# A decoder step with a mixture of experts: each expert block adds its gated rows to h by an accumulating scatter, and the closing stage keeps only the last norm

## The chip, the cores and the metric

One core of a Trainium2 chip runs the whole program. The metric is the device time of one execution in microseconds; the median of the runs counts. In the profile PE is the matmul engine (PEld its weight load), DVE the vector engine, ACT the scalar engine, POOL the GpSimd engine and SP the queue that issues plain DMAs; SPq, POOLq and so on are the instruction queues of these engines. L1835 is line 1835 of the kernel before.

## What is computed

The step is one decoder layer for 1,024 prompt tokens and 32 sample tokens (T = 1,056 rows of D = 1,024 float32), and a last norm. The part that the change touches is the mixture of experts and what follows it:

```python
def hier_moe(h, ...):
    ...
    top_v, top_i = lax.top_k(jax.nn.softmax(le, axis=-1), TOP_K)      # TOP_K = 2
    gate = g_p[:, None] * top_v / jnp.sum(top_v, axis=-1, keepdims=True)
    ...
    def expert_block(args):
        e, tok = args
        xb = x_pad[tok]
        hmid = jax.nn.silu(xb @ w_gate[e]) * (xb @ w_up[e])
        return hmid @ w_down[e]
    out = lax.map(expert_block, (blk_expert, buf_tok.reshape(n_blocks, MOE_BLOCK)))
    out = out.reshape(n_rows, D_MODEL) * buf_w[:, None]
    y = jax.ops.segment_sum(out, buf_tok, num_segments=n_tok + 1)[:n_tok]
    ...
h = h + hier_moe(rms_norm(h, norm_ffn_w), ...)
y_prompt, y_sample = rms_norm(h, norm_final_w)
```

Each token goes to 2 of 32 experts, which gives 2,112 assignments. An expert's rows are padded to blocks of 128, and the program makes at least one block for every expert; with these inputs there are 32 blocks (the trace shows 32 gathers and 32 scatters), so of 4,096 block rows 2,112 hold an assignment.

## The kernel before, in words

**Stages.** `front` (L129) computes everything up to the router: it stores h and its normed copy hn to DRAM scratch, and leaves on chip the gates (`S["gate"]`, 128 x 9 x 2), the one-hot choice of experts, each token's rank within its expert, and `S["place"]`, 18 matrices of 128 x 128 (one for each tile of 128 tokens and each of its two choices) that put an assignment on its row of a block. It also loads the first expert's weights. Then come `experts` (L1710) and `combine` (L2096). Between two such stages all engines meet at the end of a block of the program.

**The tables** are made at the start of `experts`. DVE works out in which block an assignment lies (`in_block`, 128 x 18 x 50), PE sums `place` times `in_block` over the 18 matrices (L1901, in the float32r type, one recorded matmul each), and the sum holds token + 1 in the rows of a first choice, -(token + 1) in those of a second, and 0 in an unfilled row. Seven DVE operations, six of them waiting for the one before (L2023 to L2030), turn this into two integer tables: row 0 the token to gather, with a number past the end for an unfilled row, and row 1 the row of `picked` to scatter to. L2032 copies the expert of every block. Each `table_ready` or `rows_ready` count lets the other engines go on.

**The loop over blocks.** The weights of an expert are 4 pieces `wgu` of 1 MB (gate and up) and 4 pieces `wd` of 0.5 MB (down). Every product is made of three float32r products, of high and low parts: ACT casts a piece to its high part (L1928, L1934), DVE subtracts to get the low part (L2048, L2057). There is one buffer for `wgu` and one for `wd`, so SP issues the load of the next expert's piece (L1785, L1792) when DVE has made the low part of the piece there. For a block i PE runs 48 matmuls of 512 columns for gate and up, turns the next block's tokens (L1859), runs 24 matmuls for down of block i - 1, and turns the hidden rows of block i (L1879). DVE copies the finished rows of block i - 1 from PSUM to `yb` (L2042, `unload_y`); PE may start the next down product only after that. The last block uses banks 4 and 5 and the tile `xg` in place of `yb` (L2088).

**GpSimd's queue** holds, in the order of the program: the gather of tokens for block i + 2 into `xg` (L1823 copies the column of row numbers to `src`, L1826 is the indirect DMA; it waits until PE has turned the tokens before), then the scatter of block i - 1 (L1832 copies the column to `dst`, L1835 is the indirect DMA from `yb` to the scratch tensor `picked`, 2T rows, one for each choice of each token). Row numbers past the end are skipped. The copy at L1832 waits until the scatter before has landed, and so does DVE's next write of `yb` (L2040).

**The end.** SP loads the last norm's weight and, while the last blocks compute, h itself: four tiles to `h_final` (L1804) and five to `h_late` (L1807). It waits for the last scatter (L1808), and the stage ends. `combine` then loads the two rows of each token from `picked` (L2126, nine DMAs, 8.65 MB), adds gate times row to h, for tiles 8, 0, 2, 4, 6 on DVE (L2186) and for tiles 1, 3, 5, 7 on PE with diagonal matrices of gates (L2209, L2148 to L2150), squares and sums on ACT (L2171 or L2165), takes the root (L2172, L2168), multiplies by its reciprocal and the weight on DVE (L2196, L2203, L2200), and stores from GpSimd's queue (L2134).

Of the kernel before, what the change touches and what calls it, by code (L numbers as in the profile page):

```python
# [6 lines left out]
ALU = mybir.AluOpType  # L7
# [3 lines left out]
I32 = mybir.dt.int32  # L11
# [1698 lines left out]
def experts(nc, A, S, C, bank):  # L1710
# [3 lines left out]
    with ExitStack() as ctx:  # L1714
# [44 lines left out]
        x_high, h_high = sem("xb_high"), sem("h_high")  # L1759
        silu_done, hid_ready = sem("silu_done"), sem("hid_ready")  # L1760
        xT_psum, xT_done = sem("xTb_psum"), sem("xTb_done")
        hT_psum, hT_done = sem("hT_psum"), sem("hT_done")
        y_done, y_stored = sem("y_done"), sem("y_stored")
# [10 lines left out]
        def _(sp):  # L1774
# [27 lines left out]
            sp.wait_ge(rows_ready, 1)  # L1802
            for j in range(FIRST):
                sp.dma_start(S["h_final"][:, j, :], S["h"][j * P:(j + 1) * P, :]).then_inc(S["final_loaded"][j], 16)  # L1804
            sp.wait_ge(gu_split, m * 4 + 8)
            for t in range(FIRST, NT + 1):
                sp.dma_start(S["h_late"][0:rows_of(t), t - FIRST, :], S["h"][t * P:t * P + rows_of(t), :]).then_inc(S["final_loaded"][t], 16)  # L1807
            sp.wait_ge(y_stored, m * 16 + 32)  # L1808
            sp.sem_inc(holder, 1)

        @block.gpsimd
        def _(pool):
# [4 lines left out]
                                    in_offset=bass.IndirectOffsetOnAxis(ap=of_row[:, 0, 0:1], axis=0),  # L1817
# [3 lines left out]
            def gather(i):  # L1821
                wait(pool, xg_loaded, i * 16)
                then_own(pool, nc.gpsimd.tensor_copy(src[:], of_row[:, 0, bass.ds(i, 1)]), src_ready, i)  # L1823
# [6 lines left out]
            def scatter(i):  # L1830
                wait(pool, y_stored, i * 16)
                then_own(pool, nc.gpsimd.tensor_copy(dst[:], of_row[:, 1, bass.ds(i, 1)]), dst_ready, i + 1)  # L1832
                pool.wait_ge(y_done, i + 1)
                pool.sem_inc(holder, 1)
                pool.indirect_dma_start(out=S["picked"], out_offset=bass.IndirectOffsetOnAxis(ap=dst[:], axis=0),  # L1835
                                        in_=yb[:], in_offset=None, bounds_check=2 * T - 1, oob_is_err=False).then_inc(y_stored, 16)

            gather(1)
            gather(2)
            with pool.Fori(1, m + 1) as i:  # L1840
                gather(i + 2)
                scatter(i - 1)
            scatter(m)
            scatter(m + 1)
            last = m + 2
# [484 lines left out]
```

## Time and profile before

| | us |
|---|---|
| median of 3 runs | 1507.23 (1505.0 to 1507.36) |
| profiled execution | 1505.11 |
| its span in the profile | 1503.4 |
| PE busy in the span | 1416.1 (94%) |
| DVE busy | 1061.5 (71%) |
| ACT busy | 766.1 (51%) |
| POOL busy | 568.4 (38%) |

The program's order in the span: `front` to about 861 us, the tables to 875 us, the loop over blocks to about 1456 us, the last scatter, and `combine` to the end. An engine's busy time doesn't count queue instructions. "DMA share" is the mean busy share of the core's 16 DMA engines; where packets overlap it can pass 1. "PEclk" is the matmul engine's granted clock as a share of full speed.

### The profile page before, as it was taken

To read this page: it belongs to the slowest core of one execution; us is meant where nothing else is said; L and a number is where in the kernel's file an instruction comes from. 1 tells how busy PE (TensorE), PEld (TensorE's weight loads), DVE (VectorE), ACT (ScalarE), POOL (GpSimd) and SP (SyncE) were. 2 spreads that over 40 slices of the span, in tenths; PEclk is the share of its full clock that TensorE was granted. 3 is DMA by queue.
4 is the path that set the end of the run, shared out by engine and by line. 5 is a ranking of instruction groups with operands and counts; after the bars stand their busy time and mean duration, and the time that the engine had idled before them with its cause. 6 is when DMAs were issued, how large, how long until landed. Compare 5 with 4: busy or idle time off the path is not lost. (4 is left out here: it accounts for less than half of the span.)

```text
span 1503.4 us, 21686 instructions
## 1 busy us (share of the span) xinstructions
PE 1416.1 (94%) x7625; PEld 1233.0 (82%) x7625; DVE 1061.5 (71%) x1225; ACT 766.1 (51%) x891; POOL 568.4 (38%) x345
## 2 busy tenths in 40 slices
PE   6999999999999999899999659999999999999976
PEld 5999999999999998788877548888888888888852
DVE  6687722366666664545463579999999999999956
ACT  6332222333333335344433438777777777777734
POOL 2323324454444442485644014333433333333311
PEclk9999999999999999999999669999999999999997
DMA  5222333234444445876653659999999999999958
GB/s 197 65 78 86 126 95 111 80 130 143 144 141 147 138 144 167 294 219 239 209 168 130 231 201 383 402 396 390 377 381 362 389 379 383 385 388 387 369 211 343
DMA packets 115793, 361.07 MB, mean 240 GB/s; under 512 B 18772, under 2 KB 48468, under 8 KB 99348
## 3 DMA queue, kind: packets, MB, share of 16 engines
q1 hardware_dynamic: 100164, 322.37, 58.6%
q0 software_dynamic: 15568, 37.87, 7.3%
q8 instruction: 41, 0.67, 0.2%
q14 instruction: 20, 0.16, 0.0%
HBM read 316.52 MB, written 59.64 MB: 250 GB/s over the span
## 5 line engine op out<-in xcount | busy, mean ns | idle before, releaser
L2048 DVE TENSOR_TENSOR wgu_l<-wgu,wgu_h 128x2048 fp32r<-128x2048 f32 x128 | 290.0, 2288 | 27.4 <-ACT wgu_h L1928 26.5
L1928 ACT CAST wgu_h<-wgu 128x2048 fp32r<-128x2048 f32 x124 | 237.4, 1915 | 100.6 <-PE bank0and L64 100.5
L62 PE MATMUL bank0and<-wgu_h,xh_blk 128*128 128x512 f32 x512 | 203.7, 398 | 2.9 <-DVE xl_blk L2052 2.9
L64 PE MATMUL bank0and<-wgu_h,xl_blk 128*128 128x512 f32 x512 | 200.9, 392 | 0.0
L62 PE MATMUL bank0and<-xh,wh 128*128 128x352 f32 x576 | 197.6, 343 | 3.0 <-ACT raw L906 3.0
L63 PE MATMUL bank0and<-wgu_l,xh_blk 128*128 128x512 f32 x512 | 200.3, 391 | 0.0
L64 PE MATMUL bank0and<-xh,wl 128*128 128x352 f32 x576 | 186.7, 324 | 0.0
L63 PE MATMUL bank0and<-xl,wh 128*128 128x352 f32 x576 | 186.5, 324 | 0.0
L1671 POOL TENSOR_TENSOR wol<-wo,woh 128x1024 fp32r<-128x1024 f32 x48 | 121.4, 2536 | 123.5 <-ACT woh L996 123.5
L1835 POOL DMA_INDIRECT scratch_picked<-yb,dst x31 | 92.7, 2991 | 197.5 <-DVE yb L2042 197.5
L2057 DVE TENSOR_TENSOR wd_l<-wd,wd_h 128x1024 fp32r<-128x1024 f32 x128 | 148.2, 1219 | 1.2 <-ACT wd_h L1934 1.0
L1622 POOL TENSOR_TENSOR wl<-w,wh 128x1024 fp32r<-128x1024 f32 x36 | 87.7, 2437 | 155.7 <-ACT wh L893 155.7
L1934 ACT CAST wd_h<-wd 128x1024 fp32r<-128x1024 f32 x128 | 124.9, 1049 | 1.7 <-PE bank2and L64 1.7
L62 PEld LDWEIGHTS bank0and<-wgu_h,xh_blk 128*128 128x128 f32 x512 | 96.8, 189 | 22.7 <-issue 2.8
L62 PEld LDWEIGHTS bank0and<-xh,wh 128*128 128x128 f32 x576 | 109.7, 190 | 6.9 <-issue 5.6
L64 PEld LDWEIGHTS bank0and<-wgu_h,xl_blk 128*128 128x128 f32 x512 | 96.6, 189 | 20.8
L63 PEld LDWEIGHTS bank0and<-wgu_l,xh_blk 128*128 128x128 f32 x512 | 96.9, 189 | 19.4
L63 PEld LDWEIGHTS bank0and<-xl,wh 128*128 128x128 f32 x576 | 110.0, 191 | 2.6 <-issue 1.9
L64 PEld LDWEIGHTS bank0and<-xh,wl 128*128 128x128 f32 x576 | 109.3, 190 | 0.0
L1191 DVE COPY stage<-bank2and 128x512 f32<-128x512 f32 x26 | 18.0, 692 | 123.3 <-PE bank2and L568 123.3
L915 ACT ACTIVATE feat<-bank0and 128x352 f32<-128x352 f32 x48 | 22.1, 463 | 156.1 <-PE bank0and L64 156.0
L62 PE MATMUL bank2and<-wd_h,hT_h 128*128 128x512 f32 x248 | 99.3, 401 | 0.0
(496 smaller groups left out, 3234.5 us busy)
## 6 DMA issues: line engine op xcount, KB each, us to landing
wgu<-in_w_gate_up SPq DMA_DIRECT2D x128, 1024.0 KB, 7.6
wd<-in_w_down SPq DMA_DIRECT2D x128, 512.0 KB, 7.6
wo<-in_w_out SPq DMA_DIRECT2D x48, 512.0 KB, 4.9
w<-in_w_in_tiles SPq DMA_DIRECT2D x36, 512.0 KB, 3.6
yy<-scratch_picked SPq DMA_DIRECT2D x8, 1024.0 KB, 12.6
scratch_xb<-stage POOLq DMA_DIRECT2D x10, 512.0 KB, 4.0
xb<-scratch_xb SPq DMA_DIRECT2D x8, 640.0 KB, 4.4
scratch_uT<-feat SPq DMA_DIRECT2D x8, 528.0 KB, 5.0
```

What stands on the lines that cost most here:

```text
L62: nc.tensor.matmul(acc, lh, rh, start=start, stop=False)
L63: nc.tensor.matmul(acc, lh, rl, start=False, stop=False)
L64: return nc.tensor.matmul(acc, ll, rh, start=False, stop=stop)
L915: nc.scalar.activation(feat[q % 2][:, b * TB:(b + 1) * TB], bank[b][:, 0:TB], func).then_inc(acc_free, 1)
L1191: ins = nc.vector.tensor_copy(stage[j][:, 4 * g:4 * g + 4, :], bank[3 + g][:].rearrange("p (t c) -> p t c", t=4))
L1622: nc.gpsimd.tensor_tensor(wl[q % 2][:], w[q % 2][:], wh[q % 2][:].bitcast(F32), ALU.subtract).then_inc(w_split, 1)
L1671: nc.gpsimd.tensor_tensor(wol[n % 3][:], wo[n % 3][:], woh[n % 3][:].bitcast(F32), ALU.subtract).then_inc(w_split, 1)
L1835: pool.indirect_dma_start(out=S["picked"], out_offset=bass.IndirectOffsetOnAxis(ap=dst[:], axis=0), in_=yb[:], in_offset=None, bounds_chec ...
L1928: nc.scalar.copy(wgu_h[:, s], wgu[:, s]).then_inc(gu_high, 1)
L1934: nc.scalar.copy(wd_h[:, p, :], wd[:, p, :]).then_inc(down_high, 1)
L2048: nc.vector.tensor_tensor(wgu_l[:, s], wgu[:, s], wgu_h[:, s].bitcast(F32), ALU.subtract).then_inc(gu_split, 1)
L2057: nc.vector.tensor_tensor(wd_l[:, p, :], wd[:, p, :], wd_h[:, p, :].bitcast(F32), ALU.subtract).then_inc(down_split, 1)
```

## The change

The second table and the scratch tensor `picked` go. h in DRAM gets 128 spare rows. One table of row numbers serves gather and scatter: token for a filled row, T + partition for an unfilled one. A table of gates for each row of each block is built beside it: DVE multiplies `in_block` by the gates (128 x 900), PE sums `place` times that over 18 float32 matmuls of 49 columns, and DVE divides by the token's signed number. GpSimd copies the column of gates of each block to `gate_of` (`copy_gate`), DVE multiplies by it where it copied before (`add_h`), and the scatter adds into h. All 128 rows of each block are written. `add_h` of the last block, which had waited for PE alone, also waits for the scatter before, and the last scatter too. After the last scatter SP loads h, nine tiles, and `combine` is square, root, reciprocal, product and store, with the stores on SP.

```diff
@@ experts: tiles
-        of_row = own("of_row", [P, 2, MAXBLK], I32)
+        of_row = own("of_row", [P, MAXBLK], I32)
+        gate_of, past_end = own("gate_of", [P, 1]), own("past_end", [P, 1])
+        gate_row = at("gate_row", 190208, [P, MAXBLK])
+        in_gate = at("in_gate", 182016, [P, N_ASG, WIDE])
@@ SP
-            sp.wait_ge(rows_ready, 1)
-            for j in range(FIRST):
-                sp.dma_start(S["h_final"][:, j, :], S["h"][j * P:(j + 1) * P, :]).then_inc(S["final_loaded"][j], 16)
             sp.wait_ge(gu_split, m * 4 + 8)
-            for t in range(FIRST, NT + 1):
-                sp.dma_start(S["h_late"][0:rows_of(t), t - FIRST, :], S["h"][t * P:t * P + rows_of(t), :]).then_inc(S["final_loaded"][t], 16)
             sp.wait_ge(y_stored, m * 16 + 32)
             sp.sem_inc(holder, 1)
+            for t in range(NT + 1):
+                sp.dma_start(S["h_final"][0:rows_of(t), t, :], S["h"][t * P:t * P + rows_of(t), :]).then_inc(S["final_loaded"][t], 16)
@@ GpSimd
+            def copy_gate(i):
+                wait(pool, y_done, i)
+                pool.sem_inc(holder, 1)
+                nc.gpsimd.tensor_copy(gate_of[:], gate_row[:, bass.ds(i, 1)]).then_inc(gate_copied, 1)
+
-            def scatter(i):
+            def scatter(i, rows=yb):
                 wait(pool, y_stored, i * 16)
-                then_own(pool, nc.gpsimd.tensor_copy(dst[:], of_row[:, 1, bass.ds(i, 1)]), dst_ready, i + 1)
+                pool.sem_inc(holder, 1)
+                then_own(pool, nc.gpsimd.tensor_copy(dst[:], of_row[:, bass.ds(i, 1)]), dst_ready, i + 1)
                 pool.wait_ge(y_done, i + 1)
                 pool.sem_inc(holder, 1)
-                pool.indirect_dma_start(out=S["picked"], out_offset=bass.IndirectOffsetOnAxis(ap=dst[:], axis=0),
-                                        in_=yb[:], in_offset=None, bounds_check=2 * T - 1, oob_is_err=False).then_inc(y_stored, 16)
+                pool.indirect_dma_start(out=S["h"], out_offset=bass.IndirectOffsetOnAxis(ap=dst[:], axis=0),
+                                        in_=rows[:], in_offset=None, bounds_check=T + P - 1, oob_is_err=True,
+                                        compute_op=ALU.add).then_inc(y_stored, 16)
             gather(1)
+            pool.wait_ge(table_ready, 3)
+            nc.gpsimd.tensor_copy(gate_of[:], gate_row[:, 0:1]).then_inc(gate_copied, 1)
             gather(2)
             with pool.Fori(1, m + 1) as i:
                 gather(i + 2)
                 scatter(i - 1)
+                copy_gate(i)
             scatter(m)
+            copy_gate(m + 1)
             scatter(m + 1)
-            last = m + 2
...
+            copy_gate(m + 2)
+            scatter(m + 2, xg)
@@ PE
+            pe.wait_ge(blk_ready, 2)
+            for a in range(N_ASG):
+                r = P if a < 2 * NT else TS
+                last = nc.tensor.matmul(bank[2][:, 0:MAXBLK], S["place"][0:r, a, :].bitcast(F32), in_gate[0:r, a, 0:MAXBLK], start=(a == 0), stop=(a == N_ASG - 1))
+            last.then_inc(blk_psum, 1)
             pe.wait_ge(rows_ready, 1)
             m = blocks_but_three(pe) + 1
             turn_x(0)
@@ DVE: the tables
+            after(nc.vector.tensor_scalar(past_end[:], C["row_no"][:], float(T + 1), None, ALU.add))
             dve.wait_ge(rows_psum, 1)
-            signed = of_row_f[:, 1, :]
+            signed, other, number = (of_row_f[:, j, :] for j in range(3))
             after(nc.vector.tensor_copy(signed, bank[0][:, 0:MAXBLK]))
...
+            after(nc.vector.tensor_scalar(other, signed, 0.0, past_end[:], ALU.is_equal, ALU.mult))
+            after(nc.vector.scalar_tensor_tensor(out=number, in0=signed, scalar=-1.0, in1=signed, op0=ALU.mult, op1=ALU.max))
+            nc.vector.scalar_tensor_tensor(out=of_row[:], in0=number, scalar=-1.0, in1=other, op0=ALU.add, op1=ALU.add).then_inc(rows_ready, 1)
             dve.wait_ge(blk_psum, 1)
             nc.vector.tensor_copy(blk_i[:, 0:MAXBLK], bank[1][0:1, 0:MAXBLK]).then_inc(table_ready, 1)
+            flat_gate = S["gate"][:].rearrange("p t k -> p (t k)")
+            nc.vector.tensor_tensor(in_gate[:], in_block[:].bitcast(F32), flat_gate.unsqueeze(2).to_broadcast([P, N_ASG, WIDE]), ALU.mult).then_inc(blk_ready, 1)
+            dve.wait_ge(rows_ready, 1)
+            after(nc.vector.tensor_scalar(other, signed, 0.0, None, ALU.is_equal))
+            after(nc.vector.tensor_tensor(other, other, signed, ALU.add))
+            after(nc.vector.reciprocal(other, other))
+            dve.wait_ge(blk_psum, 2)
+            nc.vector.tensor_tensor(gate_row[:], bank[2][:, 0:MAXBLK], other, ALU.mult).then_inc(table_ready, 1)
@@ DVE: the loop, and the last block
-            def unload_y(i):
+            def add_h(i, rows=yb, banks=S["banks23"]):
+                dve.wait_ge(gate_copied, i + 1)
                 wait(dve, y_stored, i * 16)
                 dve.wait_ge(down_used, i * 4 + 4)
-                nc.vector.tensor_copy(yb[:], S["banks23"][:]).then_inc(y_done, 1)
+                nc.vector.tensor_scalar(rows[:], banks[:], gate_of[:], None, ALU.mult).then_inc(y_done, 1)
...
-            dve.wait_ge(down_used, (m + 1) * 4 + 4)
-            nc.vector.tensor_copy(xg[:], S["banks45"][:]).then_inc(y_done, 1)
+            add_h(m + 1, xg, S["banks45"])
@@ combine: SP, ACT and DVE; what PE and GpSimd did goes
+            for t in range(NT + 1):
+                sp.wait_ge(out_ready, t + 1)
+                dst = A["y_sample"] if t == NT else A["y_prompt"][t * P:t * P + P, :]
+                sp.dma_start(dst, h[0:rows_of(t), t, :]).then_inc(out_stored, 16)
+            sp.wait_ge(out_stored, 16 * (NT + 1))
...
+                act.wait_ge(S["final_loaded"][t], 16 if t else 32)
+                after(nc.scalar.activation(junk[0:r, t % 2, :], h[0:r, t, :], ACT.Square, accum_out=st[0:r, t, 0:1]))
+                nc.scalar.activation(st[0:r, t, 1:2], st[0:r, t, 0:1], ACT.Sqrt, bias=C["eps"][0:r, :], scale=1.0 / D).then_inc(rms, 1)
...
+                dve.wait_ge(S["final_loaded"][t], 16 if t else 32)
+                dve.wait_ge(rms, t + 1)
+                after(nc.vector.reciprocal(st[0:r, t, 2:3], st[0:r, t, 1:2]))
+                nc.vector.scalar_tensor_tensor(out=h[0:r, t, :], in0=h[0:r, t, :], scalar=st[0:r, t, 2:3], in1=w[0:r, :],
+                                               op0=ALU.mult, op1=ALU.mult).then_inc(out_ready, 1)
@@ scratch
-    "h": (T, D), "hn": (T, D), "picked": (2 * T, D),
+    "h": (T + P, D), "hn": (T, D),
```

## Rows read from the trace of the kernel before

**Rows 1.** Busy time by stretch: span, busy us (instructions) of PE, PEld, DVE, ACT, POOL; PEclk, DMA share, GB/s.

```profile
1206.30:1312.60 106.30, 106.30 (x505) 88.47 (x504) 101.98 (x73) 80.71 (x67) 37.33 (x24) 1.00 0.99 382
1226.00:1229.54 3.54, 3.54 (x18) 2.92 (x17) 3.54 (x3) 2.23 (x2) 2.73 (x1) 1.00 1.03 418
1444.00:1450.00 6.00, 6.00 (x31) 4.95 (x29) 3.59 (x4) 4.13 (x5) 0.34 (x1) 1.00 1.02 415
...
1459.00:1503.40 44.40, 23.44 (x48) 10.01 (x48) 27.16 (x40) 15.80 (x40) 4.91 (x10) 0.73 0.77 299
```

**Rows 2.** DMA view of 1206.3 to 1312.6 us, six blocks: packets, MB, share of 16 engines.

```profile
DMA packets 8614, 40.63 MB, mean 382 GB/s; under 512 B 1744, under 2 KB 1744, under 8 KB 5566
...
q0 software_dynamic: 1728, 3.08, 7.6%
```

**Rows 3.** Timeline of POOL, one turn of the loop: start us, us, instruction, idle before.

```profile
1244.53 2.83 POOL L1835 DMA_INDIRECT scratch_picked<-yb,dst  x1 [6.50 <-DVE yb L2042]
1247.35 1.34 POOL L1823 COPY src<-of_row 128x1 int32 x1
1251.37 1.04 POOL L1826 DMA_INDIRECT xg<-scratch_hn,src  x1 [2.67 <-PE bank4and L1859]
1255.53 0.20 POOL L1832 COPY dst<-of_row 128x1 int32 x1 [3.12 <-DMA scratch_picked<-yb,dst]
```

**Rows 4.** Timeline of DVE, its next write of `yb` after that scatter.

```profile
1260.15 1.22 DVE L2042 COPY yb<-bank2and 128x1024 f32<-128x1024 f32 x1
```

**Rows 5.** Short float32 matmuls: busy time by stretch, timeline of the router's, durations of L1904.

```profile
863.00:876.00 13.00, 4.60 (x20) 4.14 (x20) 10.01 (x37) 0.00 (x0) 1.37 (x2) 0.50 0.00 2
...
848.07 3.63 PE L764 MATMUL bank0and<-w_router,hnT 128*128 128x36 f32 x16
...
L1904 PE MATMUL bank0and<-ident,blk_col x2: 238/257/276, 872.9 to 872.9; 49*1 49x49 f32 x2
```

**Rows 6.** Timeline from the tables to the first product of the loop.

```profile
866.17 0.78 DVE L1992 TENSOR_TENSOR in_block<-column_no,of_block 128x600 fp32r<-128x600 f32 x1
...
874.43 0.21 DVE L2030 CAST of_row<-of_row_f 128x98 int32<-128x98 f32 x1
...
875.71 6.70 DVE L2048 TENSOR_TENSOR wgu_l<-wgu,wgu_h 128x2048 fp32r<-128x2048 f32 x3 [0.97 <-DVE blk_i L2032]
...
883.08 1.23 DVE L2052 TENSOR_TENSOR xl_blk<-bank4and,xh_blk 128x1024 fp32r<-128x1024 f32 x1 [0.67 <-ACT xh_blk L1939]
...
884.45 0.77 PE L62 MATMUL bank0and<-wgu_h,xh_blk 128*128 128x512 f32 x1 [2.45 <-DVE xl_blk L2052]
```

**Rows 7.** Timeline of DVE and POOL at the last block, and a stretch after it.

```profile
1455.98 1.22 DVE L2088 COPY xg<-bank4and 128x1024 f32<-128x1024 f32 x1 [2.07 <-PE bank4and L64]
...
1458.05 0.97 POOL L1849 DMA_INDIRECT scratch_picked<-xg,src  x1 [4.10 <-DVE xg L2088]
...
1460.50:1461.00 0.50, 0.00 (x0) 0.00 (x0) 0.00 (x0) 0.00 (x0) 0.00 (x0) 0.50 0.33 131
```

**Rows 8.** The chain that ended last: its first DMA issue, its long transfer, its last issue.

```profile
1464.55 0.32 SPq L2126
...
1469.61 20.77 DMA yy<-scratch_picked
...
1499.12 0.53 POOL out_y_prompt L2134
```

**Rows 9.** The loads of h (ns min/median/max), then the timeline of ACT and DVE in `combine`.

```profile
L1804 SPq DMA_DIRECT2D h_final<-scratch_h x4: 423/444/707, 1438.9 to 1440.6; - x4
...
1474.29 1.28 ACT L2172 ACT_TABLE_LOAD   x1
1475.58 0.29 ACT L2172 ACTIVATE st_f<-st_f,eps 32x1 f32<-32x1 f32 x1
...
1476.95 0.29 ACT L2172 ACTIVATE st_f<-st_f,eps 128x1 f32<-128x1 f32 x1
...
1493.11 1.29 DVE L2203 SCALAR_TENSOR_TENSOR h_late<-h_late,st_f,w_final 128x1024 f32<-128x1024 f32 x1
```

More of the change, by code:

```diff
@@ L1759, in experts @@
         x_high, h_high = sem("xb_high"), sem("h_high")
+        gate_copied = sem("gate_copied")
         silu_done, hid_ready = sem("silu_done"), sem("hid_ready")
@@ L2075, in block_of @@
                 if not first:
-                    unload_y(i - 1)
+                    add_h(i - 1)
                 low_hid(i)
@@ L2123, in _ @@
         def _(sp):
-            for t in (8, 1, 0, 3, 2, 5, 4, 7, 6):
-                r = rows_of(t)
-                sp.dma_start(yy[t][0:r], S["picked"].rearrange("(k t) d -> t k d", k=2)[t * P:t * P + r]).then_inc(loaded[t], 16)
-        @block.gpsimd
-        def _(pool):
-            for n, t in enumerate(ORDER):
-                r = rows_of(t)
-                pool.wait_ge(out_ready, n + 1)
-                dst = A["y_sample"] if r == TS else A["y_prompt"][t * P:t * P + r, :]
-                pool.dma_start(dst, h[t][0:r, :]).then_inc(out_stored, 16)
-            pool.wait_ge(out_stored, 16 * (NT + 1))
-        def psum_of(t, half):
-            return bank[2 * (ON_PE.index(t) % 4) + half]
-        @block.tensor
-        def _(pe):
-            pe.wait_ge(diag_ready, 2 * len(ON_PE))
-            for n, t in enumerate(ON_PE):
-                pe.wait_ge(loaded[t], loaded_at[t])
-                for half in range(2):
-                    s = slice(half * 512, (half + 1) * 512)
-                    acc = psum_of(t, half)[:, :]
-                    nc.tensor.matmul(acc, C["ident"][:], h[t][:, s], start=True, stop=False)
-                    nc.tensor.matmul(acc, diag[:, n, 0, :], yy[t][:, 0, s], start=False, stop=False)
-                    nc.tensor.matmul(acc, diag[:, n, 1, :], yy[t][:, 1, s], start=False, stop=True).then_inc(pe_summed, 1)
+            for t in range(NT + 1):
[3 more added lines that the diff above has]
+            sp.wait_ge(out_stored, 16 * (NT + 1))
         @block.scalar
@@ L2265, in program @@
             S[name] = [ctx.enter_context(nc.semaphore(f"{name}{p}")) for p in range(parts)]
-        S["gu_high"] = ctx.enter_context(nc.semaphore("gu_high"))
+        for name in ("gu_high", "y_stored"):
+            S[name] = ctx.enter_context(nc.semaphore(name))
         front(nc, A, S, C, bank)
         S["w_final"] = at("w_final", 190464, [P, D])
-        S["h_final"] = at("h_final", 174080, [P, FIRST, D])
-        S["h_late"] = at("h_late", 0, [P, NT + 1 - FIRST, D])
-        late = [ctx.enter_context(nc.semaphore(f"f_loaded{t}")) for t in (4, 5, 7, 6)]
-        first = [ctx.enter_context(nc.semaphore(f"final_loaded{j}")) for j in range(FIRST)]
-        S["final_loaded"] = first + [late[0], late[1], late[3], late[2], first[1]]
+        S["h_final"] = at("h_final", 0, [P, NT + 1, D])
+        S["final_loaded"] = [ctx.enter_context(nc.semaphore(f"final_loaded{t}")) for t in range(NT + 1)]
         experts(nc, A, S, C, bank)
```

88 lines of the change are left out of this document (10 added, 78 removed).

## The prediction

> **What bounds the kernel now.** I read the busy time by stretch first, since the change touches three stages with different limits: the tables, the loop, the end. In the loop PE is busy for 106.30 of 106.30 us at the full clock [rows 1], so a block costs what PE's matmuls cost: six blocks in 106.3 us, 17.72 us each. But the DMA share in that row is 0.99, at 382 GB/s. I asked next whether the DMA engines have room. When they are plainly full (share over 1) they move 418 GB/s in the loop and 415 GB/s later, where both queues are mixed [rows 1]. Six blocks moved 40.63 MB, 6.77 MB each, of which the software queue (GpSimd's gathers and scatters) had 3.08 / 6 = 0.51 MB [rows 2]. At 418 GB/s 6.77 MB take 16.2 us. So the room is about 1.5 us a block, no more. That is the figure on which this change hangs.
>
> The end is another matter. From 1459 us the matmul engine matters little, and the chain that ended last runs from SP's issues at 1464.55 through the loads of `picked` (20.77 us) to the last store [rows 8]: this stage waits for its 8.65 MB.
>
> **The change, part by part.** The sum is made against the profiled execution, 1505.11 us, which is 2.1 us below the median of 1507.23.
>
> *Tables: +8.4 us.* Four chained DVE operations stand before `rows_ready` in place of seven. They take about 0.24 us each, so the row numbers are ready 0.7 us earlier than the end of the cast at 874.64 [rows 6]: 873.9. Then the copy of the experts (0.2), and the product of `in_block` with the gates: 600 elements took 0.78 us [rows 6], 900 about 1.1, which gives 875.2. PE now has 18 float32 matmuls, and they stand in its queue ahead of the turn of the first tokens. A float32 matmul is two records (L1904: one call, x2) and short ones take 3.63 / 16 = 0.227 us a record at the half clock, which is what PE was granted there [rows 5]. So 36 x 0.227 = 8.2 us, to 883.4. DVE's queue waits for their sum before `gate_row` (0.2), and behind that wait stand the three low parts that began at 875.71 after 0.97 us [rows 6]. They begin at about 884.6 and the low part of x follows at once, at 891.4 in place of 883.08: the 0.67 us for which it had waited for ACT is gone, as x is turned by 886. PE's first product starts then at 892.8 in place of 884.45 [rows 6], and every later step hangs on it: the weight loads of the next block wait for DVE's low parts. If the clock were at its full level, the matmuls would take half as long and the cost would be 4.3 us.
>
> *Loop, engines: 0.* DVE multiplies by a column instead of copying from PSUM, both 1,024 elements; I take 1.22 us for it too [rows 4], and DVE has 106.30 - 101.98 = 4.3 us idle in six blocks [rows 1] for a little more. GpSimd gets one more copy of a column, after the scatter, where a copy took 1.34 us; it then idled 2.67 us before the gather [rows 3]. The copy fits in that idle time. Were that cover gone, the gather would be late by 1.3 us, and it has several. `add_h` waits for a gate copied some 13 us before.
>
> *Loop, scatter: +0.37 us a block, the term that decides.* Before, a scatter wrote its filled rows only, 2,112 / 32 = 66 rows, 0.27 MB. Now all 128 rows are read from `yb` and written: 0.52 MB, that is 0.26 MB more. And each of these rows of h must be fetched from DRAM to be added to: 0.52 MB more. No row of the trace shows an accumulating DMA, so I bound it. Lower end: the fetch is free; 7.03 MB at 418 GB/s are 16.8 us, under 17.72, cost 0. Upper end: each fetched byte occupies the 16 engines as a loaded byte does, at the rate of the mixed stretch (415) with no better overlap than today: today 17.72 us hold 6.77 MB at a share of 0.99, so 7.55 MB could need 7.55 / 0.382 = 19.8 us, +2.0 a block. I take the fetched bytes as full ones, since they pass the same engines, and the full rate of the loop's own row: 7.55 MB / 418 GB/s = 18.09 us, +0.37 a block. The loads that compete run from the first scatter at about 926 us to the last `wgu` load at 1415, 28 blocks: +10.4 us.
> The Trainium skill, "Collectives: The Full Stack", section "The bandwidth ceiling: the fold count and why AG ≠ RS ≠ AR", says that a reducing transfer halves the rate because the add needs two source reads on one ring. By that rule the fetched bytes count in full, which gives the same sum; if a fetch were free the total would be 10 us lower. No row here shows it.
>
> *Scatter, landing: 0, with little margin.* DVE may write `yb` again when the scatter has landed. One scatter was issued at 1244.53 and had landed by 1255.53, 11.0 us later; the next write of `yb` came at 1260.15 [rows 3, 4]. So it may take 15.6 us. With twice the rows and the fetch (0.78 MB more over 16 engines that alternate with the weight loads: 1.9 us alone, some 3 in company) it lands after 13 to 14 us.
>
> *End: -12.5 us.* The last `add_h` must wait for the scatter before it, issued some 3.5 us ahead of the last copy at 1455.98 [rows 7]; with 128 added rows I let it start 1.3 us later. The last scatter was issued at 1458.05 and its data went until 1461.0 [rows 7]; its double volume and fetch add 1.3 us, so it lands at about 1464.0 in place of 1461.4. SP's next issue was at 1464.55 [rows 8], so leaving a stage cost 3.1 us. Now SP issues nine loads of h first, 0.44 us each [rows 9], to 1468.1, then 3.1 us: `combine` begins at 1471.2. The loads (4.3 MB, 10.4 us at 415 GB/s) keep ahead of ACT. ACT needs 1.37 us a tile (1475.58 to 1476.95) plus the table load of 1.28 once [rows 9]: first root at 1473.9. DVE then norms nine tiles at 1.29 us plus a short reciprocal, 1.4 each: 1486.5. The old end came 4.3 us after its last issue at 1499.12 [rows 8]; the same gives 1490.9 in place of 1503.4. The loads of `picked`, DVE's adds and PE's 48 matmuls are gone. The loads of h now lie open, where they had been hidden under the last blocks; that is in the sum.
>
> Together +8.4 + 10.4 - 12.5 = +6.3 us: 1511.4 for the profiled execution, 1513.5 against the median.
>
> **The rivals.** *A, the additions hide (faster).* If fetches are cheap, or the engines fill their gaps better than 418 GB/s says, the loop stays at 17.72 us and 8.4 - 12.5 = -4.1 is left: 1503. For it: 1.5 us of room, and the room needed is 0.6 (rows alone) to 1.9 us (rows and fetch). Against it: with the fetch the loop would have to average 426 GB/s, more than either full stretch [rows 1]. It decides from a transfer time of 17.72 us a block on.
> *B, the scatter lands too late (slower).* If an added row costs an engine a whole trip to DRAM that nothing overlaps, the landing passes 15.6 us, DVE waits for `yb`, and PE waits for it. Each microsecond beyond costs 30 us in all: 17 us would give 1503 + 42 = 1545. For it: only about 2 us of margin. Against it: eight rows for each engine are few.
> *C, the tables cost less.* If PE's clock rises during the 8 us of short matmuls, the tables cost 4 to 6 us. The stretch of short router matmuls at 848 us stayed at half clock to its end [rows 5], so I give it little. With the forecast's loop it gives 1510; with A's 1500.
> *D, it doesn't do what it says:* were unfilled rows still dropped as tiny packets, the loop would stay as it is, with A's time.
>
> **How the numbers follow.** A measurement of this kernel can tell about 0.2%, 3 us, from no change: below 1504.2 is faster, above 1510.2 slower. The forecast's own case (the loop grows by 0.1 to 0.8 us a block, 1506 to 1526) has 0.42, of which a quarter falls within 0.2%. A has 0.33 with D; of it 0.24 is faster, the rest within, as its -4.1 us is close to the bound. B, with the upper end of the transfer cost, has 0.18. C has 0.07, split over all. Faster 0.27, same 0.21, slower 0.52. The range goes from 1500 (A with a cheap table) to 1540 (the transfer at +1.2 us a block, or a landing of 17 us). Its own range for the likeliest case is 1506 to 1526.
>
> **What would show it.** The step between two writes of `yb`: 17.7 us for A, 18.0 to 18.5 for the forecast, with DMA share at 1.0 or over, and ACT's waits for weights (today for PE alone). For B: DVE idle before `add_h`, ended by the scatter. In the DMA view of six blocks the software queue should show at least 0.78 MB a block in place of 0.51, and fewer packets under 512 B. The first product of the loop should start at about 893 us, after 36 short matmul records that take 8 us. The stretch from the last product to the end should be 12 us shorter. The forecast is wrong if the loop's step is unchanged, or if GpSimd's gather makes PE wait.

## The result, and the profile after

The changed kernel took 1521.37 us (median of 4 runs, 1519.61 to 1522.66) against 1506.22 for the kernel before (4 runs). The ratio is 1.0100, with a 95% interval of 1.0082 to 1.0117: slower by 15 us. The profiled execution of the changed kernel spans 1519.6 us, 16.2 more than the 1503.4 of before. The direction was forecast and the time lies in the range, but the forecast had +6.3 us, less than half of what came.

I cut both executions at two points that every kernel of this study has: the start of the loop's first product (PE, L62) and the end of the last product of its last block (PE, L64; 1455.56 + 0.39 us in the kernel before).

| us | first product | loop, to the last product's end | from there to the end | span |
|---|---|---|---|---|
| before | 884.45 | 571.50 | 47.45 | 1503.4 |
| after | 891.71 | 592.46 | 35.43 | 1519.6 |
| difference | +7.26 | +20.96 | -12.02 | +16.2 |
| forecast | +8.4 | +10.4 | -12.5 | +6.3 |

So the miss is in the loop. These are three stretches of the changed kernel's busy time by stretch (columns as in [rows 1]), six blocks of the loop and two parts of the end:

```profile
1212.60:1325.20 112.60, 108.62 (x503) 87.80 (x503) 103.86 (x73) 81.41 (x67) 41.27 (x31) 1.00 1.03 376
...
1484.00:1496.00 12.00, 0.16 (x1) 0.00 (x0) 1.28 (x1) 0.00 (x0) 1.74 (x2) 0.71 0.46 79
1496.00:1519.60 23.60, 0.00 (x0) 0.00 (x0) 12.28 (x18) 13.39 (x28) 0.00 (x0) 0.50 0.94 367
```

Six blocks take 112.6 us in place of 106.3, and PE, which had been busy in all of them [rows 1], is idle for 4.0 us. The DMA share rose from 0.99 to 1.03, yet the engines move 376 GB/s where they moved 382. They are full, with less to show for it. The DMA view of 1239 to 1345 us in the changed kernel says which queue fills them:

```profile
DMA packets 8102, 39.99 MB, mean 377 GB/s; under 512 B 1242, under 2 KB 1242, under 8 KB 5199
...
q1 hardware_dynamic: 6603, 35.94, 83.3%
q0 software_dynamic: 1499, 4.06, 19.0%
...
wgu<-in_w_gate_up SPq DMA_DIRECT2D x22, 1024.0 KB, 14.3
wd<-in_w_down SPq DMA_DIRECT2D x24, 512.0 KB, 16.2
scratch_h<-yb,dst POOLq DMA_INDIRECT x6, 9.2
```

The software queue has 19.0% of the engines' time for 4.06 MB; before it had 7.6% for 3.08 MB [rows 2]. The bytes of rows fetched to be added to are not in this count. And the weight pieces take 14.3 and 16.2 us from issue to landing, in the kernel before 8.4 and 7.9 over the same stretch. The waits of ACT in the same stretch, in us, times, longest, show that they now land too late:

```profile
ACT wd_h L1947 <- DMA wd<-in_w_down: 15.7, 17, 1.5
ACT wgu_h L1941 <- DMA wgu<-in_w_gate_up: 13.3, 18, 1.0
```

In the kernel before, ACT waited at `wgu_h` for PE alone (20.7 us in six blocks, a buffer still in use). The loop's bound has passed from PE to the DMA engines. The step between two writes of `yb` says the same. This is the timeline of the changed kernel's DVE, two of its writes:

```profile
1243.41 1.28 DVE L2061 TENSOR_SCALAR yb<-bank2and,gate_of 128x1024 f32<-128x1024 f32 x1
...
1262.18 1.28 DVE L2061 TENSOR_SCALAR yb<-bank2and,gate_of 128x1024 f32<-128x1024 f32 x1
```

That is 18.77 us. The first three steps are still 17.7 us, the next ten 18.0 to 18.8, and the fifteen from 1168 us on 18.7 to 19.0: the loads start with a lead and lose it. The kernel before has 17.71 us from its third step on.

### The profile page after: what moved, and what is told of

The parts are those of the page before. It is cut to its first block and busy times, and to the rows that moved or that the text cites. A ratio compares the mean times of both kernels' runs of the same rounds, so it can differ in the third digit from the quotient of the medians.

```text
span 1519.6 us, 21757 instructions
## 1 busy us (share of the span) xinstructions
PE 1410.4 (93%) x7613; PEld 1231.0 (81%) x7613; DVE 1057.6 (70%) x1206; ACT 769.2 (51%) x879; POOL 567.1 (37%) x368
## 3 DMA queue, kind: packets, MB, share of 16 engines
q0 software_dynamic: 14368, 41.66, 11.3%
## 5 line engine op out<-in xcount | busy, mean ns | idle before, releaser
L62 PE MATMUL bank0and<-wgu_h,xh_blk 128*128 128x512 f32 x512 | 204.6, 400 | 16.9 <-DVE xl_blk L2071 16.9
L64 PE MATMUL bank0and<-wgu_h,xl_blk 128*128 128x512 f32 x512 | 201.0, 393 | 0.0
L62 PE MATMUL bank0and<-xh,wh 128*128 128x352 f32 x576 | 197.5, 343 | 2.9 <-ACT raw L906 2.9
L64 PE MATMUL bank0and<-xh,wl 128*128 128x352 f32 x576 | 186.6, 324 | 0.0
L1947 ACT CAST wd_h<-wd 128x1024 fp32r<-128x1024 f32 x128 | 133.3, 1053 | 72.2 <-DMA wd<-in_w_down 67.5
L2076 DVE TENSOR_TENSOR wd_l<-wd,wd_h 128x1024 fp32r<-128x1024 f32 x128 | 153.4, 1223 | 12.2 <-ACT wd_h L1947 11.3
L1842 POOL DMA_INDIRECT scratch_h<-yb,dst x31 | 58.9, 1901 | 207.7 <-DVE yb L2061 207.7
L62 PEld LDWEIGHTS bank0and<-wgu_h,xh_blk 128*128 128x128 f32 x512 | 96.8, 189 | 42.1 <-DVE xl_blk L2071 15.3
L62 PEld LDWEIGHTS bank0and<-xh,wh 128*128 128x128 f32 x576 | 109.5, 190 | 6.9 <-issue 5.5
L64 PEld LDWEIGHTS bank0and<-wgu_h,xl_blk 128*128 128x128 f32 x512 | 97.0, 189 | 20.8
L64 PEld LDWEIGHTS bank0and<-xh,wl 128*128 128x128 f32 x576 | 109.2, 190 | 0.0
L62 PE MATMUL bank2and<-wd_h,hT_h 128*128 128x512 f32 x248 | 99.3, 401 | 0.0
```

Source lines behind the costliest of these rows:

```text
L62: nc.tensor.matmul(acc, lh, rh, start=start, stop=False)
L64: return nc.tensor.matmul(acc, ll, rh, start=False, stop=stop)
L1842: pool.indirect_dma_start(out=S["h"], out_offset=bass.IndirectOffsetOnAxis(ap=dst[:], axis=0), in_=rows[:], in_offset=None, bounds_check=T ...
L1947: nc.scalar.copy(wd_h[:, p, :], wd[:, p, :]).then_inc(down_high, 1)
L2076: nc.vector.tensor_tensor(wd_l[:, p, :], wd[:, p, :], wd_h[:, p, :].bitcast(F32), ALU.subtract).then_inc(down_split, 1)
```

## The experiments

All are edits of the changed kernel. The kernel before took 1505.84 us beside e1 to e4 and 1505.65 beside e5, e8, e9 and e10. I tell them in the order of the argument. The stages, cut as above, in us:

```
                                            first    loop    end    span
                                            product
after: adds, all 128 rows                   891.71  592.46  35.43  1519.6
e1  plain write, all 128 rows               891.54  571.84  29.52  1492.9
e3  plain write, filled rows                892.22  571.81  29.47  1493.5
e2  adds, filled rows                       891.70  587.83  35.77  1515.3
e4  adds, all rows; 8% less weights         892.03  571.84  35.53  1499.4
e10 adds, all rows, spread                  893.00  581.28  35.82  1510.1
e8  adds, filled rows, spread               892.63  571.64  34.03  1498.3
e5  as after, gate sums in two parts        882.42  593.83  35.95  1512.2
e9  e8 + e5 + one wait less                 884.35  571.34  33.31  1489.0
```

### e1 and e3: the same scatter without the addition

```diff
-            in_=rows[:], in_offset=None, bounds_check=T + P - 1, oob_is_err=True,
-            compute_op=ALU.add).then_inc(y_stored, 16)
+            in_=rows[:], in_offset=None, bounds_check=T + P - 1, oob_is_err=True).then_inc(y_stored, 16)
```

e3 has this and in place of the bounds `bounds_check=T - 1, oob_is_err=False`, by which the rows past the tokens are dropped. Both leave out the addition to h: a row overwrites what stands there.

> The scatter writes all 128 rows but adds nothing (plain write over h, so what h held is lost and the outputs differ): the fetch of h's rows is taken away, the spare rows stay. Theory (the 16 DMA engines are full, and the fetch fills them): 6.55 MB of loads and gathers and 0.52 MB written are 7.07 MB, 16.9 us at 418 GB/s, under PE's 17.7; the step between two writes of yb goes from 18.77 to 17.72 us, the time falls by about 21 us in the loop and 3 to 5 us at the end, to 1495 to 1498. Rival (the spare rows themselves or their number are what costs): the step stays over 18.3 us and the time over 1510.

> Plain write and only the filled rows: the scatter of the kernel before, inside the changed kernel (the addition is left out, so the outputs differ). What then remains of the change is the tables (+7.8 us) and the end. Theory: step 17.72 us, the end some 4 to 6 us shorter than in the changed kernel since both last scatters land 3 us sooner, 1494 to 1497. Rival (the gate copy on GpSimd, the multiply on DVE or the later gather make the loop longer): the step stays above 18 us with this scatter too.

Measured: e1 1495.27 us, ratio to the kernel before 0.9933 (0.9912 to 0.9954); e3 1495.58, ratio 0.9939 (0.9922 to 0.9957). The DMA view of e1 from 1239 to 1345 us:

```profile
DMA packets 8638, 42.35 MB, mean 400 GB/s; under 512 B 1368, under 2 KB 1368, under 8 KB 5570
...
q1 hardware_dynamic: 6910, 37.73, 90.0%
q0 software_dynamic: 1728, 4.62, 10.9%
```

The rows themselves are free: 128 rows a block or only the filled ones, the loop takes 571.8 us, though e1 moves 400 GB/s. Its software queue needs 10.9% for 4.62 MB, where the adding one needs 19.0% for less. The addition costs the whole 20.6 us of the loop and 5.9 us of the end. The duration of one packet of that queue with 4,096 bytes, from the trace's packet records of 1200 to 1420 us, has a median of 159 ns in e1 and in the kernel before, and of 327 ns in the changed kernel, where two thirds of these packets are added rows. A row that is added costs an engine 2.06 times a row that is written.

### e2: adds, but only the filled rows

```diff
-            in_=rows[:], in_offset=None, bounds_check=T + P - 1, oob_is_err=True,
+            in_=rows[:], in_offset=None, bounds_check=T - 1, oob_is_err=False,
```

> The scatter adds, but skips the unfilled rows (numbers past the end are dropped), so 66 rows a block are fetched and written on average. In the changed kernel the software queue took 20.0% of the engines for 112.6 us in six blocks, 3.75 us a block, of which a scatter about 3.1. Theory: half the rows cost half, 1.6 us; 15.7 + 1.6 = 17.3 us is just under 17.7, the step is 17.7 to 17.9 us, the time 1495 to 1501. Rival (an accumulating scatter costs by its existence, as a wait or a slow queue, not by its bytes): the step stays at 18.3 us or more and the time over 1510.

Measured: 1517.02 us, ratio 1.0079 (1.0062 to 1.0096). I had expected that half the added rows would take the loss with them (1495 to 1501 us); the gain over the changed kernel is 4 us. From its DMA view of 1239 to 1345 us, and its busy time in that stretch:

```profile
q1 hardware_dynamic: 6624, 35.76, 86.4%
q0 software_dynamic: 1614, 2.95, 11.9%
```

```profile
1239.00:1345.00 106.00, 103.03 (x482) 83.71 (x481) 98.27 (x69) 77.68 (x62) 41.49 (x30) 1.00 0.98 365
```

The mean share fell to 0.98, below that of the kernel before, and PE still idles 3 us in 106. Its late steps are 18.77 us, as in the changed kernel. So the engines are not full on average, and something about them is full all the same.

The 16 completions of one load, one from each DMA engine, say what. From the trace's completion records: the median over the first down piece of each block, landed between 1200 and 1420 us, sorted, in us after the first of the 16.

```
before 0 0  .1 .1 .1 .2 .2 .2 | .8  .9  1.1 1.2 1.4 1.4 1.9  2.6
after  0 .1 .2 .3 .5 .5 .7 .9 | 1.4 3.3 4.9 5.1 5.2 6.7 6.9 10.0
e2     0 0  .1 .1 .1 .2 .4 .5 | .9  1.1 1.3 1.5 2.0 3.4 5.2 10.1
e8     0 0  .1 .2 .3 .4 .4 .5 | .5  .7  .8  1.3 1.5 1.7 2.2  2.7
e4     0 0  .1 .2 .3 .5 .7 .7 | 1.1 1.1 1.2 1.3 1.3 1.4 1.4  2.9
e10    0 .1 .2 .4 .5 .5 1.1 1.4 | 2.7 2.8 5.1 5.2 7.7 8.8 9.4 9.7
```

In the changed kernel and in e2 half of the engines are early together, the others come late, and the last one 10 us behind. The width alone doesn't name the cause: it is 10 us wherever the loop waits for its loads (e10 too) and 2.6 to 3.5 wherever PE sets the pace (e4 too, with the changed kernel's rows on the same partitions). What it says is that some engines run behind. Of the rows of a block, those that are filled stand on the partitions 0 to n - 1, 66 of them on average. If half of the engines serve the partitions 0 to 63, the first 64 rows of each gather, and in e2 of each scatter, fall to those.
The Trainium skill, "DMA: Bandwidth & Descriptors", section "The descriptor swizzle", says just that of a full tile's rows, four partitions to each engine in turn: the engines 0 to 7 serve the partitions 0 to 63 and 8 to 15 the rest. The trace agrees in the last scatter of the program, which has the engines nearly to itself. Its block has 73 filled rows (e2 has 73 packets of 4,096 bytes there). By four partitions in turn, 8 engines hold 8 of them each, 2 hold 4, 1 holds one and 5 none. The 16 completions, in us after the issue, fall into just these groups:

```
rows           none, 5 engines    one  four     eight, 8 engines
e3 plain       2.0 2.0 2.0 2.1 2.1 | 2.2 | 2.6 2.6 | 3.1 3.1 3.2 3.2 3.2 3.2 3.2 3.2
e2 adds        2.7 2.7 2.7 2.7 2.7 | 3.2 | 4.5 4.7 | 5.5 5.8 5.8 5.8 6.0 6.0 6.3 6.4
```

In e8, told below, the same 73 rows alternate between the halves; then 14 engines should hold 4 or 5 and two 8. Its completions are 14 from 4.2 to 4.8 us and two at 5.7 and 6.4.

So the **fullest engine** may set the pace, not their mean. Its load is counted from packets and their durations in the trace: for each block 32 packets of 8,192 bytes of `wgu` at 309 ns and 32 of 4,096 bytes of `wd` at 159 ns, 15.0 us on every engine. On the fullest engine of the first half come 8 gathered rows (1.27 us) and 8 scattered ones (1.27 plain, 2.62 added):

```
            weights  gather  scatter   fullest engine   late step measured
before       15.0     1.27    1.27         17.5             17.71
after        15.0     1.27    2.62         18.9             18.77
e1           15.0     1.27    1.27         17.5             17.71
e2           15.0     1.27    2.62         18.9             18.77
e3           15.0     1.27    1.27         17.5             17.71
```

PE's own matmuls need 17.71 us, so that is the step wherever the engine needs less. The table was made after these runs, from their packets; it is a theory until it forecasts something. The sum takes medians; the means of the 8,192-byte packets lie at 311 to 346 ns, which would add up to 1.2 us, so the differences between the lines carry more weight than the last tenths.

e2's loop is 4.6 us shorter than the changed kernel's with the same late step: it has that step only from 1258 us on, and 16.9 to 19.0 until then. The filled rows of each block fit this. Counted from the tiny packets of each gather's dropped rows, they run from 24 to 110 (2,112 in sum). By four partitions in turn the first engine has its full 8 rows from 36 filled ones on. Only five blocks have fewer (24, 35, 28, 30, 28), all of them between the twelfth and the seventeenth, and all blocks from the eighteenth on have 38 or more. There e2's steps stay at 18.76 to 18.8 from 1276 us until the loads run out, though the filled rows change from 38 to 87: it is the fullest engine's count that holds still, not the mean.

### e4: fewer weight bytes beside the same added rows

```diff
-                    sp.dma_start(wd[:, p, :], A["w_down"][e, p * P:(p + 1) * P, :]...
+                    cols = slice(0, D if p < 3 else 64)
+                    sp.dma_start(wd[:, p, cols], A["w_down"][e, p * P:(p + 1) * P, cols]...
```

It leaves out 960 of the 1,024 columns of each block's fourth down piece (its columns keep old values).

> The scatter stays as changed; of the fourth down piece only 64 of 1,024 columns are loaded (the rest of the tile is stale, so the outputs differ): 0.49 MB less of plain loads a block, 1.2 us of all engines at 418 GB/s. Theory (full DMA engines set the step): the step falls by 1.05 us to 17.7 to 17.8 us, the time to 1499 to 1503. Rival (the landing of the scatter, GpSimd's order or DVE's waits set it): the step stays at 18.77 us and the time at 1521, as none of these is touched.

Measured: 1502.27 us, ratio 0.9979 (0.9969 to 0.999). The loop is at PE's 571.84 us again, with every row added. From the waits of ACT in e4 from 1239 to 1345 us, the only one for this buffer:

```profile
ACT wgu_h L1942 <- PE bank0and L64: 19.9, 19, 1.6
```

The loss in the loop is a lack of DMA time, and not the landing of the scatter, nor the extra operations on DVE and POOL, all of which e4 still has. By the fullest engine: eight packets of 159 ns become eight of 18, so 18.9 less 1.1 is 17.8, for PE's 17.71.

### e8 and e10: the rows of a block spread over all partitions

Rank r of a block is put on partition 64 (r mod 2) + r/2 by a permuted row of column numbers; a constant of its own keeps the numbers of the blocks.

```diff
+    done(nc.gpsimd.iota(C["column_no"][:].rearrange("p (a b) -> p a b", a=2), [[1, 2], [2, P // 2]], ...
+    done(nc.gpsimd.iota(C["block_no"][:], [[1, WIDE]], ...
...
-                nc.vector.tensor_tensor(in_block[:, a0:a1, :], C["column_no"][:, 0:WIDE]...
+                nc.vector.tensor_tensor(in_block[:, a0:a1, :], C["block_no"][:]...
```

e8 also drops the unfilled rows as e2 does; e10 adds all 128.

> As the run that adds only filled rows, but an assignment of rank r goes to partition 64*(r mod 2) + r/2 instead of partition r. In that run 66 filled rows of 128 still gave steps of 18.77 us although the software queue's share fell from 19.7% to 11.7%, and eight of the sixteen completions of a weight load came up to 10 us after the other eight. Theory (the filled rows lie on partitions 0 to 65, which one half of the 16 DMA engines serves, and the fullest engine sets the step): each engine now has 15.0 us of weight loads, 4 gathered rows at 0.16 and 4 added rows at 0.33 us, 17.0 us in all; the step falls to 17.71 us and the completions close up; 1497 to 1502 us. Rival (an accumulating scatter holds all engines up, whatever rows it has): steps of 18.77 us remain, 1515 or more.

> The changed kernel with that spread of ranks over partitions, all 128 rows still added. The scatter was balanced already; the gather becomes so. Theory of the fullest engine: 15.0 + 4 x 0.16 + 8 x 0.33 to 0.36 = 18.3 to 18.5 us, so the step falls from 18.77 to 18.3 to 18.5, not to 17.7; 1511 to 1517 us. Rival (the mean over the engines counts): nothing changes, 18.77 us and 1521.

Measured: e8 1500.24 us, ratio 0.9963 (0.9949 to 0.9978); e10 1510.07, ratio 1.0032 (1.0021 to 1.0044). The DMA view and the busy time of e8 from 1239 to 1345 us:

```profile
DMA packets 8629, 40.87 MB, mean 386 GB/s; under 512 B 1725, under 2 KB 1725, under 8 KB 5557
...
q0 software_dynamic: 1728, 3.16, 11.9%
```

```profile
1239.00:1345.00 106.00, 106.00 (x504) 88.22 (x503) 102.10 (x73) 80.41 (x67) 36.32 (x31) 1.00 1.02 386
```

e8 issues the same rows, packets and additions as e2; only the partitions differ. PE is busy in all of 106 us at a mean DMA share of 1.02, where e2 lost 3 us at 0.98. Its last completion comes 2.7 us after the first, about as before the change. That is the test of the theory: the fullest engine has 15.0 + 0.65 + 1.35 = 17.0 us (66 rows over 16 engines are 4.1), under PE's 17.71, and the step is 17.71. For e10 it gives 15.0 + 0.65 + 2.62 = 18.3 us; its steps from the eighth on are 18.0 to 18.6, 18.2 in the mean.

The sum takes 4 gathered rows on each engine, and that holds for blocks of up to 64 filled rows; from 72 on the first engine of each half has 8 again, 0.64 us more. The steps from 1112 us on show it: set beside the filled rows of the block four further on, they are 18.0 to 18.3 us for 64 rows or fewer (mean 18.05), 18.3 for the one of 68, and 18.3 to 18.6 for 73 or more (mean 18.56). I chose the shift of four because it fits; with shifts of 0 to 3 and 5 the two means differ by 0.12 at most, and not always the same way. By the same count e8 isn't even in its large blocks either, 18.9 us by the sum, and yet loses nothing: ten blocks in a row with 58 rows or fewer come before most of them, and the sum is 0.3 too high in e10. Whether it is the engines themselves that are full on that half, or their way into the memories, no run separates.

Taken together, dropping the unfilled rows alone is worth 4.4 us (1521.4 to 1517.0), spreading alone 11.3 (1510.1), both 21.1 (1500.2): spreading halves what the fullest engine gathers in blocks of up to 64 filled rows, dropping halves what it adds once the rows are spread, and alone nearly none of it.

### e5: the gate sums in two parts

```diff
-            for a in range(N_ASG):
-                ...
-            last.then_inc(blk_psum, 1)
+            sum_gates(0, 12)
...
             turn_x(0)
+            sum_gates(12, N_ASG).then_inc(blk_psum, 1)
```

`sum_gates(a0, a1)` holds the old loop's body. DVE's four operations for `gate_row`, with their wait for PE, stand behind `low_gate_up(0)` in place of ahead of it.

> The changed kernel with its gate tables moved: 12 of the 18 float32 matmuls before the turn of the first tokens (PE waits there for the gather), 6 behind it (PE waits there for the low part of x), and DVE's last four table operations behind its first low parts. Theory (DVE's wait for the matmuls is the whole +7.8 us of the tables): the first product starts at 885 to 886 us in place of 891.7 and the time falls by 6 to 7 us, to 1514 to 1516; steps as they were, 18.77. Rival (the loop, which is held by the DMA engines, takes the gain back): the first product is earlier, the time falls by less than 3 us.

Measured: 1514.43 us, ratio 1.0058 (1.0041 to 1.0074), 7 us below the changed kernel. Timeline of the changed kernel from the tables to the first product, then that of e5:

```profile
873.45 1.07 DVE L2044 TENSOR_TENSOR in_gate<-in_block,gate 128x900 f32<-128x900 f32 x1
874.58 8.08 PE L1916 MATMUL bank2and<-in_gate,place 128*128 128x49 f32 x36 [2.00 <-DVE in_gate L2044]
882.76 0.21 DVE L2050 TENSOR_TENSOR gate_row<-bank2and,of_row_f 128x49 f32<-128x49 f32 x1 [7.38 <-PE bank2and L1916]
883.73 6.70 DVE L2067 TENSOR_TENSOR wgu_l<-wgu,wgu_h 128x2048 fp32r<-128x2048 f32 x3 [0.76 <-DVE gate_row L2050]
890.34 1.22 DVE L2071 TENSOR_TENSOR xl_blk<-bank4and,xh_blk 128x1024 fp32r<-128x1024 f32 x1
...
891.71 0.77 PE L62 MATMUL bank0and<-wgu_h,xh_blk 128*128 128x512 f32 x1 [7.16 <-DVE xl_blk L2071]
```

```profile
872.73 6.69 DVE L2073 TENSOR_TENSOR wgu_l<-wgu,wgu_h 128x2048 fp32r<-128x2048 f32 x3
872.82 5.35 PE L1916 MATMUL bank2and<-in_gate,place 128*128 128x49 f32 x24 [2.00 <-DVE in_gate L2048]
...
879.70 2.80 PE L1916 MATMUL bank2and<-in_gate,place 128*128 128x49 f32 x12
...
882.42 0.79 PE L62 MATMUL bank0and<-wgu_h,xh_blk 128*128 128x512 f32 x1
```

In the changed kernel DVE stands still for 7.38 us behind PE's 36 records, and its three low parts (6.70 us) start only then. In e5 they lie beside the sums. Its front was 1.8 us earlier by itself (from `in_gate`, 873.45 against 871.69), the rest of the 9.3 us is the edit: 7.5. The loop doesn't take it back: it has 593.8 us, 1.4 more than the changed kernel's, with the same late step of 18.77. So this part of the loss adds to the other and is removed by itself.

### e9: what beats both

e8 and e5 together, and the last `add_h` no longer waits for the scatter before it: that wait guards `yb`, and the last block writes to `xg`.

```diff
-                wait(dve, y_stored, i * 16)
+                if rows is yb:
+                    wait(dve, y_stored, i * 16)
```

> All together: filled rows only, spread over the partitions, the tables split as above, and the last block's multiply no longer waits for the scatter before (it writes xg, not yb; the last scatter still waits). Theory: loop 571.8 us from first to last product, first product at 885 to 886 us, the end about 32 us: span 1489 to 1492, time 1490 to 1494, faster than before by about 1%. If the loop or the tables give back, 1496 or more.

Measured: 1491.49 us (1490.18 to 1493.37), ratio 0.9909 (0.9892 to 0.9925), so 14 us faster than the kernel before. Against e8 the first product came 8.3 us earlier and the end was 0.7 shorter. The wait was worth little (DVE idles 2.0 us before the last `add_h`, 3.4 in e8): timeline of e9's DVE and POOL at the last block:

```profile
1455.80 1.28 DVE L2069 TENSOR_SCALAR xg<-bank4and,gate_of 128x1024 f32<-128x1024 f32 x1 [2.04 <-PE bank4and L64]
...
1457.47 0.18 POOL L1840 COPY dst<-of_row 128x1 int32 x1 [3.20 <-DMA scratch_h<-yb,dst]
...
1458.52 1.56 POOL L1843 DMA_INDIRECT scratch_h<-xg,dst  x1 [0.87 <-POOL dst L1840]
...
1465.15 4.45 SPq L1811 DMA_DIRECT2D h_final<-scratch_h  x9
```

DVE starts 2.0 us after PE's last record now, in place of 5.13 in the changed kernel, but POOL's copy of `dst` still waits for the same scatter, as its indices may not change under way. A second `dst` would take that away; it was not tried. Nor was the spread in the kernel before, whose 17.5 us by the sum lie under PE's 17.71 already.

## Why the prediction was right in sign and wrong in size

**What bounds the kernel: right.** The room of the DMA engines was the figure on which the change hung, and it ran out.

**Tables, +8.4: right, +7.3.** 36 records of 8.08 us were forecast as 8.2, `in_gate` of 1.07 as 1.1, the first product at 892.8 for 891.71. The granted clock stayed at 0.50 from 874 to 885 us, which ends rival C. From the row table's copy on (DVE, 873.00 before, 872.43 after) the stage grew by 7.8 us; the rest is a front that came 0.6 us sooner.

**Loop, engines, 0: right.** The multiply takes 1.28 us, and in e1, e4 and e8 DVE's 102.1 to 102.2 us of 106.0 leave PE busy throughout. Nobody in the loop waits for GpSimd's extra copy.

**Scatter, landing: right, and rival B is out.** From the changed kernel's timeline of POOL, a turn of the loop:

```profile
1245.58 1.60 POOL L1842 DMA_INDIRECT scratch_h<-yb,dst  x1 [7.61 <-DVE yb L2061]
...
1254.86 2.12 POOL L1839 COPY dst<-of_row 128x1 int32 x1 [3.43 <-DMA scratch_h<-yb,dst]
```

It has landed 9.3 us after its issue, not in the forecast 13 to 14 (in e4, where PE sets the pace, the median is 12.3), and DVE's next write of `yb` at 1262.18 doesn't wait. With the limit at 15.6 us the cost is none.

**Scatter, +0.37 a block: this is the step that failed.** "I take the fetched bytes as full ones, since they pass the same engines, and the full rate of the loop's own row: 7.55 MB / 418 GB/s = 18.09 us, +0.37 a block." The first half held: an added row takes 327 ns against 159, the fetched bytes at full price.
The Trainium skill, "Collectives: The Full Stack", section "The bandwidth ceiling: the fold count and why AG ≠ RS ≠ AR", has a ReduceScatter run at half the rate of an AllGather because its add needs two source reads. It speaks of rings between cores; the added rows of this scatter behave alike, 327 ns for 159.
The second half did not. Megabytes over a rate is a mean over 16 engines, and a load is complete when its last engine is. The first 64 filled rows of a gather sit on eight of them, so the fullest had 18.9 us of work, not 18.1 (by packets the mean is 18.3). Measured: 20.96 us over the same 28 blocks, 0.75 a block, twice the term; the late steps lose 1.06 each. With every row added but the filled ones spread (e10) the loop grew by 581.28 - 571.50 = 9.8 us: close to the forecast's +10.4. So what it lacked is the placement; that the two agree so well is partly luck, as e10 loses next to nothing in its first steps and 0.5 us in each from the eighth on, not 0.37 in all 28. e2 had half the added rows and the same late step as the changed kernel; e8 had e2's rows, spread, and lost nothing. The bounds (0 to +2.0 a block) did hold it. The uneven load could be read before: the kernel before had half of its completions early and the last 2.6 us behind. One bound was narrower than its own words: a landing of 17 us was priced at 1545 and yet named as a reason for a range that ends at 1540. Nothing hung on it.

**Rival A** failed for the reason given against it, though with the rows spread and the empty ones dropped it is what happens: e8's loop is PE's. **Rival D** is out: packets under 512 bytes fell from 1,744 [rows 2] to 1,366 in six blocks, by 378, about six times the 62 unfilled rows that a scatter no longer drops. The gather still drops its own.

**End, -12.5: right, -12.0, partly by errors that cancel.** Timeline of the changed kernel from the last scatters to the last store:

```profile
1480.76 1.74 POOL L1842 DMA_INDIRECT scratch_h<-yb,dst  x1 [2.27 <-DVE yb L2061]
...
1483.78 0.39 PE L64 MATMUL bank4and<-wd_h,last_l 128*128 128x512 f32 x1
...
1487.32 1.28 DVE L2061 TENSOR_SCALAR xg<-bank4and,gate_of 128x1024 f32<-128x1024 f32 x1 [5.13 <-DMA scratch_h<-yb,dst]
1489.44 1.56 POOL L1842 DMA_INDIRECT scratch_h<-xg,dst  x1 [1.74 <-DVE xg L2061]
1495.75 4.31 SPq L1810 DMA_DIRECT2D h_final<-scratch_h  x9
1500.49 1.06 ACT L2143 ACTIVATE junkf<-h_final 128x1024 f32<-128x1024 f32 x1 [20.75 <-PEq L1714]
...
1503.35 0.16 DVE L2158 RECIPROCAL st_f<-st_f 128x1 f32<-128x1 f32 x1 [14.74 <-ACT st_f L2144]
...
1514.68 1.27 DVE L2159 SCALAR_TENSOR_TENSOR h_final<-h_final,st_f,w_final 32x1024 f32<-32x1024 f32 x1
1515.98 0.33 SPq L2129 DMA_DIRECT2D out_y_sample<-h_final  x1
```

The wait of the last `add_h` cost 3.1 us (5.13 in place of the 2.07 of [rows 7]), not 1.3. The last scatter's landing took 6.3 us (1489.44 to 1495.75), where the forecast had 4.7 (to 1464.0 from 1458.05 + 1.3). Against that, leaving the stage after SP's ninth load cost 0.4 us (1500.06 to 1500.49) where I had 3.1 from [rows 8]. Why those are gone is open: no kernel here tests it. ACT's and DVE's part came as forecast: 13.0 us from the first root at 1502.95 to the end of the last norm, for 12.6.

## What to carry to other kernels

Where many loads share the DMA engines, add up the packets of each engine, times their measured duration, and compare the fullest one with the bound of the loop; a mean over 16 engines hides 0.6 us a block in the changed kernel (18.3 for 18.9 by the sum) and 1.9 in e2 (17.0 for 18.9). A tile of which only the first rows are used loads half the engines here: spread the rows over the partitions, and drop those that nobody reads. Count an accumulating row as two. When a table is added on one engine's queue, look which long independent operations of another engine wait behind its result.

## What the runs showed of the hardware that I had not expected

- The completions of one 512 KB load spread over 10 us in e2 and over 2.7 in e8, which has the same rows in alternation over both halves; PE's idle time in 106 us of the loop goes from 3 us to none. The spread is a sign of a loop that waits for its loads: e10 has it too (9.7 us), and e4 doesn't (2.9).
- Sixteen completions of a scatter without company show how many rows each engine holds, in e3's and e2's last scatter to the single row.
- An addition makes the landing of that lone scatter 3 us later. From its issue to SP's first load of h: 3.4 us in e1 (128 rows, plain), 3.3 in e3 (filled, plain), and 6.3 in the changed kernel, 6.4, 6.5 and 6.6 in e2, e8 and e9 (adding, all or filled). This doesn't mean that the number of rows is without effect: the last block has 73 filled rows, and the fullest engine holds 8 in each of these runs. In e2 an engine without a row is done after 2.7 us (2.0 in e3), one with 4 after 4.6 (2.6), one with 8 after 5.5 to 6.4 (3.1 to 3.2). Some of the first packets of the changed kernel's last scatter took 0.8 to 1.4 us each, in place of 0.33.
- The fetched rows are in no count of bytes: the engines' mean share rises while the GB/s fall (1.03 at 376 against 0.99 at 382 [rows 1]). The 8.65 MB by which the whole run's reads from DRAM fell (316.5 to 307.9) are just the loads of `picked`. A fall of GB/s at a share of 1 is how the accumulating scatter looks in this profile.
